# A decoder block on one core: the channel mixer's weight sums on DVE, four operand slots, down projection in half units

## The reference, cut to what matters

```
h = rms_norm(x, norm_ffn_pre)
gate = causal_dwconv(h @ w_gate, conv_w, conv_b)      # width 3 along time
up = h @ w_up
ffn_out = (gelu(gate) * up) @ w_down
x = x + rms_norm(ffn_out, norm_ffn_post)
```

## Time and profile before

| | |
|---|---|
| median of 3 runs | 2929.03 us (2922.47 to 2929.09) |
| profiled execution | 2925.74 us, its span 2924.1 us |
| granted PE clock, mean | 0.99 |
| busy | PE 97%, DVE 57%, ACT 38%, POOL 24% |
| DMA | 300.06 MB read, 58.72 MB written |

### The profile page before, as it was taken

How to read it: one execution, slowest core, us unless ns; L and a number is a source line. 1 busy time by engine, 2 the same in 40 slices (tenths; PEclk the granted TensorE clock), 3 DMA queues, 4 the chain that set the end, 5 groups by cost and what they waited for, 6 DMA issues and landing times.

```text
span 2924.1 us, 41716 instructions
## 1 busy us (share of the span) xinstructions
PE 2834.1 (97%) x16287; PEld 2495.5 (85%) x16287; DVE 1677.9 (57%) x1508; ACT 1108.2 (38%) x1287; POOL 711.0 (24%) x438
## 2 busy tenths in 40 slices
PE   7999999999999999999869999999999999999997
PEld 6888888888888888888769989899998989899896
DVE  4332344344332233432578769696786969688697
ACT  3243443332222222222344444444444444444443
POOL 1000001000000000000143445444353544435353
PEclk9999999999999999999989999999999999999999
DMA  4234233332233334334514364636456473655645
GB/s 182 87 86 114 87 94 105 104 98 96 87 90 90 93 101 158 129 130 172 173 58 137 123 156 105 155 119 138 137 116 157 103 162 109 136 140 119 158 102 230
DMA packets 426496, 361.00 MB, mean 123 GB/s; under 512 B 10462, under 2 KB 354658, under 8 KB 423280
## 3 DMA queue, kind: packets, MB, share of 16 engines
q1 hardware_dynamic: 395552, 291.53, 32.7%
q0 software_dynamic: 26192, 58.91, 10.2%
q10 hardware_dynamic: 4608, 8.39, 0.7%
HBM read 300.06 MB, written 58.72 MB: 123 GB/s over the span
## 4 chain that ended last, share of the span: by engine, by line
PE 73%; DVE 18%; issue 6%; ACT 1%; POOL 1%; DVEq 0%; DMA 0%; ACTq 0%; SPq 0%; POOLq 0%
PE ps L512 18%; DVE op_ring L1902 9%; PE ps L515 9%; PE ps L812 7%; PE ps L737 6%; PE ps L829 5%; PE ps L831 5%; PE ps L830 5%; PE ps L816 4%; PE ps L536 3%; PE ps L537 3%; PE ps L538 3%; DVE arena L1959 2%; DVE arena L1962 2%; DVE arena L1541 1%
## 5 line engine op out<-in xcount | busy, mean ns | idle before, releaser
L1520 DVE TENSOR_TENSOR w_lo<-raw,w_hi 128x2048 fp32r<-128x2048 f32 x124 | 284.3, 2292 | 563.2 <-ACT w_hi L933 563.2
L1425 POOL TENSOR_TENSOR arena<-quad_ring 128x1024 f32<-128x1024 f32 x176 | 486.5, 2783 | 368.1 <-DVE op_ring L1902 315.5
L1902 DVE TENSOR_TENSOR op_ring<-quad_ring,op_ring 128x1024 fp32r<-128x1024 f32 x170 | 333.6, 1967 | 232.4 <-ACT op_ring L1170 232.4
L1902 DVE TENSOR_TENSOR op_ring<-arena,op_ring 128x1024 fp32r<-128x1024 f32 x220 | 384.6, 1748 | 44.6 <-ACT op_ring L1170 44.2
L812 PE MATMUL ps<-hl,op_ring 128*128 128x256 f32 x2816 | 367.7, 283 | 0.4 <-issue 0.4
L812 PEld LDWEIGHTS ps<-hl,op_ring 128*128 128x128 f32 x2816 | 351.1, 192 | 3.0 <-issue 2.6
L933 ACT CAST w_hi<-raw 128x2048 fp32r<-128x2048 f32 x124 | 236.4, 1907 | 260.9 <-PE ps L538 205.1
L1170 ACT CAST op_ring<-arena 128x1024 fp32r<-128x1024 f32 x220 | 230.8, 1049 | 247.2 <-PE ps L816 125.7
L812 PE MATMUL ps<-h,op_ring 128*128 128x256 f32 x2112 | 277.2, 284 | 6.0 <-DVE h L1894 6.0
L512 PE MATMUL ps<-h_hi,w_hi 128*128 128x512 f32 x1152 | 281.3, 397 | 1.1 <-ACT w_hi L933 1.1
L512 PE MATMUL ps<-h_lo,w_hi 128*128 128x512 f32 x1152 | 272.9, 389 | 0.0
(11 more groups left out here) (288 smaller groups left out, 3787.3 us busy)
## 6 DMA issues: line engine op xcount, KB each, us to landing
raw<-in_w_in SPq DMA_DIRECT2D x88, 1024.0 KB, 5.2
quad_ring<-in_ffn_w_gate SPq DMA_DIRECT2D x88, 512.0 KB, 4.6
quad_ring<-in_ffn_w_up SPq DMA_DIRECT2D x88, 512.0 KB, 4.5
quad_ring<-in_ffn_w_down SPq DMA_DIRECT2D x88, 512.0 KB, 5.3
down_sums<-arena POOLq DMA_DIRECT2D x160, 256.0 KB, 6.2
raw<-in_w_out SPq DMA_DIRECT2D x20, 1024.0 KB, 5.0
merge_gates<-arena ACTq DMA_DIRECT2D x32, 256.0 KB, 2.0
raw<-in_w_up_a SPq DMA_DIRECT2D x8, 1024.0 KB, 5.6
```

The costliest lines, as they stand in the source:

```text
L1425: pool.tensor_tensor(dst, quads[(4 * p + a) % QRING], quads[(4 * p + b) % QRING], ALU.subtract if q == M7 else ALU.add).then_inc(ff_sum, 1)
L1520: dve.tensor_tensor(w_lo[:, s, :], raw[:, s, :], f32(w_hi[:, s, :]), ALU.subtract).then_inc(lo_ready, 1)
L1902: dve.tensor_tensor(op_lo[(o + 1) % 3], source(o), f32(op_hi[(o + 1) % 3]), ALU.subtract).then_inc(ff_lo, 1)
```

## The change

The operations of a step are now given by lists: FIRST, MIDDLE (nine steps) and FINAL. A pair's products go M1, M4, M3, M2, M5, M7, M6. In a woven pair one down unit stands after M2 and one after M6. A unit covers two channel tiles (a group; there are 22) and one column block; it starts and stops its own accumulation, so it is copied and added to HBM by itself: four copies and four DMAs for each unit, 84 units, and the last group's four units at the end (tail) add to the loaded sums. A group's units run in the two pairs after the pair that made it; in the last step pair 2 carries four units and pair 3 none.

POOL does no tensor work in the loop, only the stores. DVE makes all five sums, each into a buffer of the slot of its operation (op_sum); the slots are four. A quarter has one buffer each (quads 0 to 3), the down weights two. Staging buffers are three for four token tiles: STAGE = (0, 1, 2, 0). The half-row sums of the start are all on DVE. Sums, gain and x come back to other places in SBUF.

```diff
--- before.py
+++ after.py
+M4, M2, M3, M5, M1, M7, M6, D0 = range(8)
+A11, A22, A21, A12 = range(4)
+PAIRS = 4
...
-BANKS = ((0, 1, 2, 3, 4, 0, 2), (5, 6, 7, 3, 4, 5, 7))
+GROUPS = FT // 2
+PRODUCTS = (M1, M4, M3, M2, M5, M7, M6)
+
+
+def woven(p):
+    d = D0 + 2 * (p % 2)
+    return [(p, q) for q in (M1, M4, M3, M2, d, M5, M7, M6, d + 1)]
+
+
+FIRST = [(0, q) for q in (M4, M2, M3, M5, M1, M7, M6)] + [(1, q) for q in PRODUCTS] + woven(2) + woven(3)
+MIDDLE = woven(0) + woven(1) + woven(2) + woven(3)
+FINAL = (woven(0) + woven(1) + [(2, q) for q in (M1, D0, M4, M3, D0 + 1, M2, M5, D0 + 2, M7, M6, D0 + 3)]
+         + [(3, q) for q in PRODUCTS] + [(4, D0 + d) for d in range(4)])
+PRODUCTS_END = len(FINAL) - 4
+OPS = len(MIDDLE)
+assert len(FIRST) % 4 == OPS % 4 == PRODUCTS_END % 4 == 0
+SLOT_FIRST = (1, 2, 0, 1, 2, 0, 1)
 TURNS = (M4, M4, M2, M2, M3, M3, M5, M5, M1, M1, M7, M7, M6, M6)
-TURN_BANKS = (4, 6, 4, 6, 4, 6, 4, 6, 4, 6, 4, 6, 6, 6)
+TURN_BANKS = (0, 6, 0, 6, 0, 2, 0, 2, 0, 2, 0, 2, 0, 0)
...
+        def sequence(i):
+            if isinstance(i, int):
+                return FIRST if i == 0 else FINAL if i == LAST else MIDDLE
+            return MIDDLE
+
+        def slot_of(i, pos):
+            return SLOT_FIRST[pos] if sequence(i) is FIRST and pos < len(SLOT_FIRST) else pos % 4
...
+        def slot_free(engine, i, pos):
+
+            earlier = [k for k in range(pos) if slot_of(i, k) == slot_of(i, pos)]
+            if earlier:
+                engine.wait_ge(ff_op, ops_before(i) + earlier[-1] + 1)
+            elif isinstance(i, int) and i == 0:
+                engine.wait_ge(unit_done, ALL_OUT - 1 if pos == 0 else ALL_OUT)
+                if slot_of(i, pos) == 3:
+                    engine.wait_ge(turned2, len(TURNS))
+            else:
+                engine.wait_ge(ff_op, ops_before(i) + pos - 3)
...
+            def load_pair(i, p):
+
+                pair = PAIRS * i + p
+                before = (i, p - 1) if p else (i - 1, 3)
+                sp.wait_ge(ff_sum, 5 * pair - 1)
+                sp.wait_ge(ff_lo, done(*before, M4))
+                load_quad(i, p, A22)
+                load_quad(i, p, A12)
+                sp.wait_ge(ff_sum, 5 * pair)
+                sp.wait_ge(ff_lo, done(*before, M3))
+                load_quad(i, p, A11)
+                load_quad(i, p, A21)
+
+            down_loads = []
+
+            def load_down(i, p, d):
+
+                if len(down_loads) < 2:
+                    sp.wait_ge(unit_done, ALL_OUT - 1)
                 else:
...
+            def gone(q):
+                sp.wait_ge(ff_op, done(LAST, 3, q))
+
+            for n in range(3):
+                sp.wait_ge(acc_added[n], 16 * (2 if n == 0 else 1) * 4 * (GROUPS - 1))
+            gone(M1)
+            for n in range(TT):
+                if n == 2:
+                    gone(M4)
+                sp.dma_start(acc[n], sums_d[n, :, :]).then_inc(acc_back[n // 2], 16)
+            gone(M5)
             sp.dma_start(z_gain, row_on_all(norm_ffn_post, 0, D)).then_inc(z_gain_loaded, 16)
-            sp.wait_ge(ff_op, OPS * LAST + 3 * PRODUCTS + M5 + 1)
             for n in range(TT):
...
+            def down(i, p, q, pos):
+
+                n_down, group = down_of(i, p, q), 2 * i + p // 2 - 1
+                o, slot, f = ops_before(i) + pos, slot_of(i, pos), 2 * (1 - p // 2)
+                w = [t[slot].rearrange("p (j n) -> p j n", j=2) for t in (op_hi, op_lo)]
+                pe.wait_ge(ff_hi, o + 1)
+                pe.wait_ge(ff_lo, o + 1)
+                pe.wait_ge(act_lo_ready, 2 * group + 2)
+                for n in range(TT):
+                    tok = slice(n * P, n * P + P)
+                    past(pe, dn_evac, 4 * n_down + n - 3)
+                    for j in range(2):
+                        pe.matmul(ps[:, n, :], act_hi[:, f + j, tok], w[0][:, j, :], start=(j == 0), stop=False)
+                        pe.matmul(ps[:, n, :], act_hi[:, f + j, tok], w[1][:, j, :], start=False, stop=False)
+                        mm = pe.matmul(ps[:, n, :], act_lo[:, f + j, tok], w[0][:, j, :], start=False, stop=(j == 1))
+                    mm.then_inc(dn_done if n < TT - 1 else ff_op, 1)
...
+
+            pe.wait_ge(dn_evac, 16 * (GROUPS - 1))
+            for part in range(2):
+                pe.wait_ge(act_lo_ready, 2 * GROUPS - 1 + part)
+                for d in range(2):
+                    if part == 0:
+                        pe.wait_ge(ff_lo, ops_before(LAST) + PRODUCTS_END + d + 1)
+                    if d == 1:
+                        pe.wait_ge(ff_half, 4 * 2 * GROUPS)
+                    tail(d, HALVES[0], (part,), nothing)
+            for e in range(2, 8):
...
+            def hi(i, pos):
+
+                i, pos = at_op(i, pos)
+                p, q = sequence(i)[pos]
+                slot = slot_of(i, pos)
+                if q in (M4, M3) or q >= D0:
+                    slot_free(act, i, pos)
+                if q >= D0:
+                    act.wait_ge(*down_loaded(i, p, q - D0))
+                    src = quads[:, 4 + (q - D0) % 2, :]
                 elif q in (M4, M3):
...
+                    part = A22 if q == M4 else A11
+                    quad_loaded(act, i, p, part)
+                    src = quads[:, part, :]
                 else:
...
+            def down_copy(i, p, q, n):
+
+                n_down, s = down_of(i, p, q), STAGE[n]
                 if n < TT - 1:
-                    act.wait_ge(dn_done, 12 * i + 3 * d + n + 1)
+                    act.wait_ge(dn_done, 3 * n_down + n + 1)
                 else:
...
+                    act.wait_ge(ff_op, done(i, p, q))
+                past(act, acc_added[s], 16 * (n_down if s else 2 * n_down + n // 3))
+                act.copy(stage[:, s, :], ps[:, n, :]).then_inc(dn_evac, 1)
+
+            def interval(i, k):
+
+                ops = sequence(i)
+                p, q = ops[k - 1] if k else (None, None)
+                if k and q >= D0:
+                    down_copy(i, p, q, 3)
+                if k + 3 < len(ops) or sequence(i) is not FINAL:
+                    hi(i, k + 3)
+                if k < len(ops) and ops[k][1] >= D0 and ops[k][0] < 4:
                     for n in range(3):
...
+                row_power(what, n)
+            pool.wait_ge(o_evac, 4 + 16)
+            pool.memset(ff_pad[:, :, 0:2], 0.0).then_inc(pad_zero, 1)
+
+            for n_down in range(4 * (GROUPS - 1)):
                 for n in range(TT):
...
+                    d, s = n_down % 4, STAGE[n]
+                    pool.wait_ge(dn_evac, 4 * n_down + n + 1)
+                    dst, src = sums_d[n, :, 512 * d:512 * d + 512], stage[:, s, :]
+                    if n_down < 4:
+                        pool.dma_start(dst, src).then_inc(acc_added[s], 16)
                     else:
...
+            def weight_sum(i, pos):
+
+                i, pos = at_op(i, pos)
+                p, q = sequence(i)[pos]
+                if q in (M4, M3) or q >= D0:
+                    return
+                a, b = {M1: (A11, A22), M2: (A21, A22), M5: (A11, A12), M7: (A12, A22), M6: (A21, A11)}[q]
+                quad_loaded(dve, i, p, a)
+                quad_loaded(dve, i, p, b)
+                slot_free(dve, i, pos)
+                dve.tensor_tensor(op_sum[slot_of(i, pos)], quads[:, a, :], quads[:, b, :],
+                                  ALU.subtract if q in (M7, M6) else ALU.add).then_inc(ff_sum, 1)
+
+            def lo(i, pos):
+
+                i, pos = at_op(i, pos)
+                q, slot = sequence(i)[pos][1], slot_of(i, pos)
+                if q >= D0:
+                    src = quads[:, 4 + (q - D0) % 2, :]
+                elif q in (M4, M3):
+                    src = quads[:, A22 if q == M4 else A11, :]
+                else:
+                    src = op_sum[slot]
+                dve.wait_ge(ff_hi, ops_before(i) + pos + 1)
+                dve.tensor_tensor(op_lo[slot], src, f32(op_hi[slot]), ALU.subtract).then_inc(ff_lo, 1)
 
...
+                    weight_sum(i, k + 3)
+                if sequence(i) is not FINAL or k + 2 < len(ops):
+                    lo(i, k + 2)
+                p, q = ops[k - 1] if k else (None, None)
+                up = k > 0 and p % 2 == 1
                 if q == M2:
...
+                    after_m2(i, p, 7 - p % 2)
                 elif q == M5:
-                    with_m5(i, p)
+                    after_m5(i, p, 6 + p % 2)
                 elif q == M7:
-                    with_m7(i, p)
+                    after_m7(i, p)
                     if up:
                         times_gate(i, p, 0)
                 elif q == M6:
-                    with_m6(i, p)
+                    after_m6(i, p)
                     if up:
                         times_gate(i, p, 1)
+                        hidden_lo(i, p, 0)
                     else:
                         taps(i, p, 0)
-                    if p == 3:
+                if k > 1 and ops[k - 2][1] == M6:
+                    p = ops[k - 2][0]
```

(62 more changed lines are left out.)

640 lines of the change are left out of this document (217 added, 423 removed).

## The result

The changed kernel took 2980.2 us (median of 4 runs) against 2925.8 us for the kernel before (4 runs): a ratio of 1.0183, 95% interval 1.0161 to 1.0204. It is slower by 54.5 us where 12 us less were forecast.

A forecast was written before the change was run, and what follows sets the result against it. PE, 97% busy, was taken to bound the kernel, with 37.4 us of stalls to win. Start -7, stalls -13.9 and tail +8.1 gave -12.8 us from 2925.7: 2912.9, taken as 2914 (own range 2900 to 2928; eight in ten 2890 to 2968).

The forecast's parts named there:

- The middle of the mixer: From the second pair's first product to the last product's end: stalls fall from 37.4 to 23.5 us, -13.9.
- Stalls after: 2.5 + 12 + 8 + 1 = 23.5: Remaining PE stalls in us: single-buffered quarters in the first step, staging-buffer waits, last step's four-unit pair, unit-product switching.
- rows 2: PE trace before the change: products 2.88 us apart, down units 5.44 us each, no gap at 1714.74 and 1758.29.
- Waits for the low part: PE's product-stage waits of about 1 us for DVE's low operand part would go, worth up to 37 us.
- The staging ring: Woven pairs: ACT's tile 3 copy waits for tile 0's store; 0.3 us in 40 pairs, 12 us.
- rival 1: Staging buffer paces PE from a mean landing of 6.9 us: 2974 us, mild form about 2940; chance 0.15.
- The signs that I had named: Failure signs: step pitch above 127.5 us, landings averaging over 6.9, or last product to span's end above 50 us.
- The last step: Its third pair carries four units, which fall behind by about 2.8 us each waiting for the buffer: 8 us.
- The start: Without POOL's sums slowing DVE, the second pair's first product comes 7.5 us earlier; taken as -7 us.
- My bound of 0: Lower bound of the gain at the start: all nine added DVE operations lie on the path.
- The tail: After the last product: less PE work, but a later gain vector holds up POOL and DVE; +8.1 us, bounds +3.8 and +14.
- Rows 9: Trace rows cited for ACT's mean times, 1.05 and 0.59 us, used to put ACT at 15 us of 31.

The follow-up runs named there:

- e1: Changed kernel with TensorE's eight middle steps written out instead of looped: 2919.7 us, ratio 1.000 to the kernel before.
- e10: Changed kernel, steps written out, each woven pair's first half down unit behind M7 instead of M2: 2958.2 us, 1.0114 to the kernel before.
- e8: Changed kernel, steps written out, the start's four half-row sums for M1 and M7 given back to POOL: 2921.1 us, 0.9988 to the kernel before.
- e11: The changed kernel with TensorE's steps written out, measured again on another chip: 2921.3 us, 0.9983 to the kernel before.
- e5: Changed kernel, still looped, with 128 long-satisfied waits put into TensorE's queue: 2929.5 us, 1.0018 to the kernel before.
- e6: The kernel before with 128 long-satisfied waits put into TensorE's queue at the same place: 2952.5 us, ratio 1.0094 to the unpadded kernel before.
- e3: Changed kernel, still looped, each accumulating store cut from 128 rows to one: 2921.4 us, 1.001 to the kernel before.
- e9: Changed kernel, still looped, but TensorE's loop jumps back three products later, between M3 and M2: 2958.6 us, 1.0111 to the kernel before.

## Why the prediction was wrong, step by step

- **The middle of the mixer.** "Stalls after: 2.5 + 12 + 8 + 1 = 23.5" left out a term. The forecast took PE's order of work as all that PE needs: its last 1 us, for all switching between unit and product, came from rows 2, where the kernel before jumps back at 1758.29 without a gap, and I took that for a property of the work. Written out (e1) the stretch has 2865.1 - 1526.6 = 1338.5 us for the same work: 14.7 us of stalls, 9 better than forecast. The missing term is the fetch of code at eight jumps: 132.3 against 124.7 us a step, 61 us, of which 39.6 us are gaps and the rest mostly half-rate matmuls behind them. The term depends on where the code ahead of the loop happens to put its head, and on the stores.
- **Waits for the low part** gone, low parts at 1.22 us, no tensor work of POOL: right. The written-out pitch of 124.7 us lies in the forecast's 124.5 to 126.
- **The staging ring** (0.3 us a pair, 12 us; rival 1 at 2940 to 2974): no wait in the middle steps. The size was wrong, the mechanism real, as e10 shows. The stores' landing is 6.7 us in the median, above the 6.2 to 6.4 of the forecast and below the 6.9 from which the ring would pace PE:
```profile
DMA to landing us min/median/max: 4.1/6.7/10.3
```
  The measured time lies just above rival 1's, for another reason. The signs that I had named, a pitch above 127.5 and a tail above 50 us, did show that the forecast failed, but not why.
- **The last step** (8 us): waits for ACT's staged copy of 0.4 + 2.4 + 0.9 + 2.1 = 5.8 us, and 1.0 us for a high part. Right within 2 us.
- **The start** (-7): 0. PE's first transposes came 4.7 us earlier (1477.85 against 1482.53) and the second 6.8 us, as worked out, and all of it was given back: 1.6 us ahead of the transposes for M1 and 3.85 us ahead of those for M7, both on half-row sums that POOL made before.
```profile
1496.01 2.20 PE L817 MATMUL ps<-ident,arena 128*128 128x128 f32 x16 [1.61 <-DVE arena L2041]
...
1504.93 3.25 PE L817 MATMUL ps<-ident,arena 128*128 128x128 f32 x16 [3.85 <-DVE arena L2048]
```
  "Those that stand ahead of M1's and M6's activations take back a few us" undercounted them. My bound of 0 was the case, and in e8 giving these sums back to POOL doesn't help either.
- **The tail** (+8.1): +16.0; in e1 21.8 + 51.3 - 58.2 = +14.9. The mechanism, a late gain vector, was right and its size was not: it took 16.6 us to land (15.3 in e1) against the 10.8 of the earlier trace rows. It landed 18 us behind the last product in e1, not 12, and DVE's first row pass starts at 2891.6, 26.5 us behind that product, where I had POOL's six gains end at 20.
- **In all** the change without the jumps is worth 0 (e1, 1.000) to 5 us (e11, 0.9983), not the 12.8 forecast: start 7 and tail 7 worse, stalls 9 better. (These terms come to 8 us, from spans on two chips on which the kernel before itself differs by 6 us.)
- **Rows 9** show groups of DVE and POOL. The forecast's means for ACT, 1.05 and 0.59 us, are those of its high part and stage copy in the same trace (1049 and 587 ns at L1170 and L1219), so that nothing hangs on it.

## What to carry to other kernels

A change that alters an engine's instruction count can move every later loop head to another place in the fetched blocks of code. Before a schedule change in a looped kernel is judged, look in the trace behind each jump for idle time that waits for no signal, and compare with the loop written out, or with some dozens of satisfied waits ahead of it. A few us an iteration can appear or vanish, and be more than the change itself. And a wait on a slow landing costs nothing as long as what is queued behind it has slack: it is the distance between the units, not the length of the wait, that counts.

## What the runs showed of the hardware

- 128 waits that are long satisfied moved one kernel by -1.6% and another by +0.94% (e5, e6). A second gap of 1.35 us with the DMA engines at 0.12 is 3.73 us with them at 0.9 or more (e3, the changed kernel).
- Two idle stretches of 2.3 and 3.7 us were followed by a granted clock at 1.2 GHz: eight low matmuls took 1.90 us instead of 1.12. In e3, idle for 1.35 us at the same place, it stayed at the upper level.
- One packet of instructions, 16 KB, went with 124 matmuls and their weight loads where TensorE's code had no jump (e1). Behind a jump PE went on 1.1 to 1.6 us after the packet for the second gap had ended (the changed kernel, e3), and 1.6 to 1.8 us after it in e9.
- Where stores kept the DMA engines busy until the jump, the packet ran as they ended, in the gap, and the gap was 2.5 to 3.6 us (e9).
